# Low halves of the weights by an adding transfer onto the negated high half

## What is computed

```python
proj = h @ w_in                      # 1024 x 3088
o    = attention(...) @ w_out        # 1024 x 1024
y    = jnp.square(jax.nn.relu(h @ w_up)) @ w_down   # 1024 x 4096, 4096 x 1024
```

## Time and profile before

| | us |
|---|---|
| median of 3 runs | 1232.93 |
| the runs | 1232.19 to 1238.27 |
| the profiled execution | 1236.35 |
| its span on the engines | 1234.4 |
| TensorE busy (matmul) | 1186.5 |
| VectorE busy | 574.4 |
| GpSimd busy | 560.2 |
| ScalarE busy | 480.9 |

### The profile page before, as it was taken

One profiled execution on the slowest core, in us unless ns is written; L12 is line 12 of the kernel. 1 busy time (PEld: TensorE's weight loads), 2 busy tenths in 40 slices (PEclk: granted clock), 3 DMA queues, 4 the chain that ended last, 5 costly groups with the idle time before them and its releaser, 6 DMA issues.

```text
span 1234.4 us, 15042 instructions
## 1 busy us (share of the span) xinstructions
PE 1186.5 (96%) x5634; PEld 984.5 (80%) x5634; DVE 574.4 (47%) x717; ACT 480.9 (39%) x594; POOL 560.2 (45%) x383
## 2 busy tenths in 40 slices
PE   6999999999999999999999789989999999999998
PEld 6887777777888888888888578767888888888887
DVE  5857868876633100234213768986643200233100
ACT  4348778864322211222224655554422111222121
POOL 4523532433665544565445602223465544455542
PEclk9999999999999999999999899999999999999999
DMA  6321121122233344233332301111333333333331
GB/s 208 97 69 35 35 68 34 34 69 69 68 102 102 102 119 150 74 99 102 102 99 72 102 1 35 35 35 44 94 102 98 97 84 95 103 102 99 99 110 34
DMA packets 142236, 101.20 MB, mean 82 GB/s; under 512 B 3128, under 2 KB 141552, under 8 KB 142192
## 3 DMA queue, kind: packets, MB, share of 16 engines
q1 hardware_dynamic: 142128, 100.56, 27.6%
q10 hardware_dynamic: 64, 0.03, 0.0%
HBM read 98.47 MB, written 2.12 MB: 81 GB/s over the span
## 4 chain that ended last, share of the span: by engine, by line
PE 67%; issue 14%; DVE 8%; POOL 6%; ACT 3%; DMA 1%; SPq 0%; POOLq 0%; ACTq 0%; DVEq 0%
PE ps L1221 21%; PE ps L1222 21%; PE ps L1223 21%; POOL w_lo L412 5%; POOL fox_sq_lo L419 1%; DVE xn_lo L864 1%; DVE rst L836 1%; DVE swa_diag L1167 1%; DVE x_hat L857 1%; ACT w_hi L471 1%; DMA x_in<-in_x 1%; ACT q_hl L733 0%; PE ps L1234 0%; DVE q_hl L1124 0%; DVE sqt L840 0%
## 5 line engine op out<-in xcount | busy, mean ns | idle before, releaser
L412 POOL TENSOR_TENSOR w_lo<-stage,w_hi 128x512 fp32r<-128x512 f32 x356 | 521.0, 1493 | 478.5 <-ACT w_hi L471 470.5
L471 ACT ACTIVATE w_hi<-stage 128x2048 fp32r<-128x2048 f32 x88 | 168.6, 1915 | 476.1 <-PE ps L1223 471.2
L1221 PE MATMUL ps<-xn_hi,w_hi 128*128 128x512 f32 x720 | 285.3, 396 | 0.3 <-issue 0.3
L1223 PE MATMUL ps<-xn_hi,w_lo 128*128 128x512 f32 x720 | 280.8, 390 | 0.0
L1222 PE MATMUL ps<-xn_lo,w_hi 128*128 128x512 f32 x720 | 280.7, 390 | 0.0
L1221 PE MATMUL ps<-r_hi,w_hi 128*128 128x512 f32 x512 | 199.8, 390 | 0.0
L1223 PE MATMUL ps<-r_hi,w_lo 128*128 128x512 f32 x512 | 199.3, 389 | 0.0
L1222 PE MATMUL ps<-r_lo,w_hi 128*128 128x512 f32 x512 | 199.2, 389 | 0.0
L1221 PEld LDWEIGHTS ps<-xn_hi,w_hi 128*128 128x128 f32 x720 | 135.5, 188 | 30.9 <-issue 2.7
L1222 PEld LDWEIGHTS ps<-xn_lo,w_hi 128*128 128x128 f32 x720 | 135.5, 188 | 29.3 <-issue 1.9
L1223 PEld LDWEIGHTS ps<-xn_hi,w_lo 128*128 128x128 f32 x720 | 135.3, 188 | 28.4
(11 more groups left out here) (207 smaller groups left out, 1610.0 us busy)
## 6 DMA issues: line engine op xcount, KB each, us to landing
stage<-in_w_up SPq DMA_DIRECT2D x32, 1024.0 KB, 5.4
stage<-in_w_down SPq DMA_DIRECT2D x32, 1024.0 KB, 5.5
stage<-in_w_in_a SPq DMA_DIRECT2D x16, 512.0 KB, 5.1
stage<-in_w_in_a SPq DMA_DIRECT2D x4, 1024.0 KB, 6.2
stage<-in_w_out_a SPq DMA_DIRECT2D x4, 1024.0 KB, 4.9
stage<-in_w_q_b SPq DMA_DIRECT2D x4, 1024.0 KB, 5.0
stage<-in_w_out_b SPq DMA_DIRECT2D x4, 1024.0 KB, 4.9
x_in<-in_x SPq DMA_DIRECT2D x4, 512.0 KB, 7.4
```

What stands on the lines that cost most here:

```text
L412: ins = nc.gpsimd.tensor_tensor(w_lo[:, s, c], stage[:, s, c], w_hi[:, s, c].bitcast(F32), ALU.subtract)
L471: nc.scalar.activation(w_hi[:, s, :], stage[:, s, :], ACT.Copy).then_inc(w_hi_ready, 1)
L1221: mm(out_, st_hi, mv_hi, start=start, stop=False)
L1223: return mm(out_, st_lo, mv_hi, start=False, stop=stop)
```

## The change

`w_lo` is made in another way. ScalarE makes two copies of `stage` instead of one: rounded to `w_hi` as before, and, by a scale of -1, negated and rounded to `w_lo`. GpSimd no longer computes: it issues one transfer of the unit from `stage` to `w_lo` that adds to its destination (SBUF to SBUF, 1 MB, float32 to fp32r), so that `w_lo` = `stage` - `w_hi`. The transfer raises `w_lo_ready` by 16, so every wait on this semaphore counts in sixteens. Ahead of each issue GpSimd waits until the transfer of the unit before has landed. GpSimd's loops over units are written out in full. Everything else, the squares' low halves included, stays.

```diff
             def slot_free(u):
 
-                after(sp, w_lo_ready, u - 1)
+                after(sp, w_lo_ready, 16 * (u - 1))
...
             def low(u, s):
+                after(pool, w_lo_ready, 16 * u)
                 pool.wait_ge(w_hi_ready, u + 1)
-                for q in range(4):
-                    c = slice(q * UNIT // 4, (q + 1) * UNIT // 4)
-                    ins = nc.gpsimd.tensor_tensor(w_lo[:, s, c], stage[:, s, c], w_hi[:, s, c].bitcast(F32),
-                                                  ALU.subtract)
-                ins.then_inc(w_lo_ready, 1)
+                pool.dma_start(w_lo[:, s, :], stage[:, s, :], accum_op=ALU.add).then_inc(w_lo_ready, 16)
...
-            with pool.Fori(0, U_PAIR // 2 + 1) as i:
+            for i in range(0, U_PAIR // 2 + 1):
                 low(2 * i, 0)
                 low(2 * i + 1, 1)
...
-                nc.scalar.activation(w_hi[:, s, :], stage[:, s, :], ACT.Copy).then_inc(w_hi_ready, 1)
+                nc.scalar.activation(w_hi[:, s, :], stage[:, s, :], ACT.Copy)
+                nc.scalar.activation(w_lo[:, s, :], stage[:, s, :], ACT.Copy, scale=-1.0).then_inc(w_hi_ready, 1)
...
-                    ins = nc.scalar.activation(w_hi[:, 1, quarter], stage[:, 1, quarter], ACT.Copy)
+                    nc.scalar.activation(w_hi[:, 1, quarter], stage[:, 1, quarter], ACT.Copy)
+                    ins = nc.scalar.activation(w_lo[:, 1, quarter], stage[:, 1, quarter], ACT.Copy, scale=-1.0)
...
-                pe.wait_ge(w_lo_ready, u + 1)
+                pe.wait_ge(w_lo_ready, 16 * (u + 1))
```

More of the change, by code:

```diff
@@ L433, in _ @@
             fox_step(1, 0)
-            with pool.Fori(1, PAIRS // 2) as t:
+            for t in range(1, PAIRS // 2):
                 fox_step(2 * t, 1)
@@ L437, in _ @@
             low(U_PAIR + PAIRS + 1, 1)
-            with pool.Fori((U_PAIR + PAIRS + 2) // 2, (U_Q + 1) // 2) as i:
+            for i in range((U_PAIR + PAIRS + 2) // 2, (U_Q + 1) // 2):
                 low(2 * i, 0)
@@ L458, in _ @@
             assert (u + 1) % 2 == 0
-            with pool.Fori((u + 1) // 2, N_UNITS // 2) as i:
+            for i in range((u + 1) // 2, N_UNITS // 2):
                 low(2 * i, 0)
@@ L1295, in proj_pair @@
                 if t == 0:
-                    pe.wait_ge(w_lo_ready, U_PAIR + i + 1)
+                    pe.wait_ge(w_lo_ready, 16 * (U_PAIR + i + 1))
                 after(pe, fox_rstd_refined, 4 * i - 3 + 2 * t)
@@ L1479, in _ @@
             s = U_KV % 2
-            pe.wait_ge(w_lo_ready, U_KV + 1)
+            pe.wait_ge(w_lo_ready, 16 * (U_KV + 1))
             wh = w_hi[:, s, :].rearrange("p (k n) -> p k n", k=KC)
```

## The result

The changed kernel takes 1291.12 us (median of 4, 1287.59 to 1292.69), the kernel before 1232.56 us: a ratio of 1.045, 95% interval [1.043, 1.048]. It is slower by 58 us. The forecast was 1377, inside 1240 to 1580: the sign and the range held, the size did not (144 us forecast, 58 measured). The profiled execution of the changed kernel is 1287.59 us with a span of 1285.8, so 51.4 us of span are to be explained.

What follows compares the result with a forecast made beforehand. TensorE, busy 96%, was taken to bound the kernel, with weight-making hidden up to 10.88 us a unit. 96 + 11 + 6 + 0 + 3 + 28 = 144 us on the profiled 1236.35 gave 1380, 1377 for the median; range 1240 to 1580.

Steps and rivals of the forecast that it cites:

- the ring: Weight units in two slots: a lag over TensorE's 10.88 us a unit pauses it before every second unit.
- L: Lag from TensorE finishing unit u-2 to unit u being ready: two ScalarE copies (3.84 us) plus X, forecast 13.8 us.
- (L + P)/2: Time per unit in dense blocks when L exceeds P, TensorE's own 10.88 us a unit.
- X: Adding transfer, issue to landing: 1.8 us fixed, two reads of 3.55, 1.0 for issue: 9.9 us; hidden below 7.04.
- Rival 1: Adding transfers at the best rate seen, 405 GB/s: X = 8.0 us, 1279 us in all; chance 0.12.
- Dense blocks: Ring pauses in both dense blocks: 1.45 us a unit over 66 units, 96 us.
- Heads: First units of each dense block ready 5.3 us later, twice: 11 us (1 to 20).
- Start and fox attention: Start: unit 1 ready later, 6 us (0 to 10); fox attention: extra copy covered by ScalarE idle time, net 0.
- Window attention: Three longer copies on the chain, 6 us, less 3 for VectorE freed from GpSimd: 3 us (-3 to +6).
- The clock: TensorE's granted clock falling after 33 pauses of 2.9 us, 1.7 us lost each; half taken, 28 us.
- Rival 2: X below 7.04 us, hidden, VectorE gains from GpSimd's freed reads: 1225 us, or 1230 to 1240; chance 0.13.
- Rival 3: Slow adding transfers, X over 14.7 us, decide each unit's time: some 1900 us at 20 us; chance 0.18.

Runs made afterwards that it cites:

- L = 11.5 and 13.5: 11.5: the changed kernel itself, 1291.12 us; 13.5: the changed kernel with ScalarE's negated copy made twice, 1390.08 us.
- plain copy: The changed kernel with the transfer copying stage onto w_lo instead of adding to it (low halves wrong): 1230.86 us.
- halves: The changed kernel with each unit made in two halves of 1024 columns, a 512 KB adding transfer behind each pair of copies: 1261.7 us.
- when it stands alone: The kernel before with ScalarE's negated copy added ahead of GpSimd's subtraction, which stays: 1259.33 us.
- the gain in window attention: The kernel before with second copy and adding transfer for units 50 to 54 alone: 1225.91 us.
- The edit of the store order: The changed kernel with the first three output stores put between the last loads on SP's queue, not behind them: 1283.47 us.

## Why the prediction was right and wrong

**Right: the ring.** Unit u starts at the later of "u-1 finished" and "u-2 finished + L", and the threshold lies between an L of 10.2 and one of 11.5, where 10.88 was put: shown by the longer periods at L = 11.5 and 13.5, and by their absence at 9 (plain copy) and 10.2 (halves). The mean of (L + P)/2 held. That the pauses fall before every second unit did not hold everywhere: stretches of both kernels have half the pause before each unit.

**Wrong: X.** This is the step that failed. It was put at 9.9 us and is 7.5 from the end of the copies: 0.53 until the issue and 6.9 to 7.0 to the landing. Of its three terms, the fixed 1.8 us came out as 1.8 for the add (1.5 for the copy). The read was mis-sized: 3.55 us for a megabyte came from the loads, whose source rows are 512 B or 1 KB in HBM; a megabyte that goes from SBUF to SBUF in 8 KB rows occupies the engines 2.6 to 2.7 us. And the issue was put at 1.0, nearly twice what it is. "Nearest to the 2 MB row" was a poor choice: the row had the bytes, but not their path. Rival 1, the best rate seen, had two reads at 5.2 us (measured 5.17) and X = 8.0; it gave 1279 us and was nearest to the measured 1291. It deserved more than 0.12.

X alone does not repair the sum. With 7.5 in place of 9.9 the forecast's own terms give L = 11.3, 15 us for the dense blocks, 6 for the heads, 3 for the start and 3 for window attention, with pauses too short for the clock: 27 us, 1260. The other 31 us to the measured 1291 are in terms that the sum had at nothing or did not have. So rival 1's 1279 is near in part by luck, too: it has 32 us for the ring's 23 and none of the places below.

The other terms of the sum, forecast and measured by the table:

- Dense blocks 96 us: 41 (7.4 + 5.8 + 3.4 + 10.8 + 13.4, a fall of the clock at unit 32 included). Of these (11.57 - 10.88)/2 x 66 = 23 are the plain ring. The rest is what the sum hadn't: the bias matrix's load beside transfers (5.8), the split that stands behind the norm's work, so that the lag there is 2 us longer (10.8 for eight units instead of 3), and single late landings.
- Heads 11 us: 4.4 + 5.3 = 9.7. The sum is near, its make-up is not: TensorE's pause there grew by 2.8 us (1.76 to 4.54) and 3.7 us (1.75 to 5.42), not by 5.3 each, and the clock, which the forecast left out here, fell at both.
- Start and fox attention 6 + 0: the start is 4.9 us late at unit 4, but VectorE's faster norm gives 4 back by unit 5; -0.5 at unit 14, ahead of which the kernel before has a fall of the clock (1.7 us) that the changed kernel has not. The claim that 2.18 us of idle cover the copy was false (0.9 us a step when it stands alone).
- Window attention +3 us: -9.5. The forecast had the mechanism and took 3 us for it. Between the high-half copies of units 50 and 56 VectorE's busy time fell from 137 to 120 us and TensorE's idle time from 19 to 12. How much of this needs the subtraction gone, and how much only its later start, is open (see the gain in window attention).
- The clock 28 us: none in the plain ring, whose pauses of 0.7 us had no fall behind them. The clock fell in or behind pauses of 3.5 us and more at the start, the heads, unit 32, in window attention (where the kernel before has falls too) and at the end; that is in their rows. In the whole profile it takes 18 us, 9 more than in the kernel before.
- The end 0 us: 9.5. The prediction followed SP's queue to the loads and called them covered. It didn't follow it to the output's stores behind the last load, nor from these to ScalarE's copy-out and the split behind that. The edit of the store order showed it.

Rival 2's gain by VectorE's freed reads was real at the start and, with the reserve above, in window attention. But X was 7.5 against a threshold of 7.04, and the 0.3 us at TensorE (its last matmul running out, the next one's start), which no term of the sum held, add to it: L is 0.6 to 0.7 us over 10.88. Rival 3 did not occur.

## What to carry to other kernels

Where a ring of slots hides a step, work out the lag at which it stops hiding and then size the step by a row of the same path (source memory, row length), not of the same bytes; here 2.8 us in one transfer lay between 0.3% faster and 4.5% slower. And put a later start of the competing work beside its removal before giving the gain to the removal. The mean place of a block is not where a longer lag hurts most: look for the places where the lag is already longer or its cover gone, heads of blocks, a large load beside it, a split behind other work, a queue that stores stand in. And a change that is worse everywhere on average can be a gain in the stage whose bound it relieves: used for 7 units of 89 it gave 0.9%.

## What the runs showed of the hardware

- An adding transfer of 1 MB from SBUF to SBUF lands after 6.9 to 7.0 us in most units, a copy after 4.2; they occupy the 16 engines for 5.17 and 2.72 us. Of two halves in flight one after the other, the first lands after 4.6 and the second after 5.7. GpSimd's instruction that issues an add takes 0.87 us, that of a copy 0.54.
- It stretches when it starts together with a load: 11.4 us at both heads (units 15 and 56, with a load of 3.5 us of all engines), 10.6 beside the 2 MB load, which itself went from 10.8 to 15.9.
- VectorE's instructions of 128x512 with two operands in SBUF take 690 ns undisturbed and some 1.7 us when they start beside a subtraction of GpSimd (1150 to 1290 ns on average in the kernel before); a whole kernel's VectorE time fell from 574 to 484 us with the subtractions. A transfer that GpSimd issues doesn't slow them so: of the changed kernel's additions for the norms 24 start while one is in flight, and none takes over 694 ns.
- Some transfers land late at the same places in every profile of the change in whole units: those of units 19, 41, 60 and 66 after 7.7 to 9.7 us. In the changed kernel's trace a load moves 0.9 and 0.7 MB beside units 19 and 60, where it is under 0.5 MB beside most. Beside 41 and 66 stands a 16 KB packet of the queue of instructions, as in the rows below (unit 66, from its issue at 1003.1 to its landing). Of the 16 transfers with such a packet in their flight 12 landed after 7.5 us or more, of the other 73 only 9. That the packet delays them was not tried.

```profile
q8 instruction: 1, 0.02, 0.7%
...
w_lo<-stage POOLq DMA_DIRECT2D x1, 1024.0 KB, 8.6
```

- A ring of two slots whose lag is over the period fixes the sum of two periods and not how it is divided: 10.94 and 13.45 us, or 12.2 and 12.2, stand in one profile.
